# The mixer's output projection as seven half-size products for each two tiles of tokens

## What is computed

```
mix = einsum('bte,ed->btd', concat([pool_out, mlstm_out], -1), w_out)   # (512+8) x 1024 @ 1024 x 1024
x   = layer_norm(ALPHA * x + mix, ln1_g, ln1_b)
```

## Time and profile before

| what | value |
|---|---|
| median of 3 executions | 668.04 us (667.41 to 669.69) |
| profiled execution | 667.49 us |
| its span, first to last instruction | 665.8 us |
| mean granted TensorE clock | 0.992 |
| busy: PE, DVE, POOL, ACT | 96%, 52%, 31%, 23% |
| output projection on PE | 248.31 to 306.40 us |

### The profile page before, as it was taken

How to read it: one execution, slowest core, us unless ns; L and a number is a source line. 1 busy time by engine, 2 the same in 40 slices (tenths; PEclk the granted TensorE clock), 3 DMA queues, 4 the chain that set the end, 5 groups by cost and what they waited for, 6 DMA issues and landing times.

```text
span 665.8 us, 8667 instructions
## 1 busy us (share of the span) xinstructions
PE 637.3 (96%) x3244; PEld 390.3 (59%) x3244; DVE 348.1 (52%) x799; ACT 152.0 (23%) x333; POOL 208.7 (31%) x245
## 2 busy tenths in 40 slices
PE   6999999999999999999999999999999999999982
PEld 3445588887787774446888774454574454333330
DVE  0283356326457792757653865355873333253445
ACT  1113221001524230002001740222324111211144
POOL 4241010100476556411101985002244342111231
PEclk9999999999999999999999999999989999999997
DMA  8994468613334345102904987454449999999698
GB/s 296 399 324 165 143 163 223 234 52 127 99 126 164 103 158 171 40 0 84 359 0 144 336 287 310 192 189 189 194 167 371 412 413 410 382 360 410 210 207 165
DMA packets 45811, 146.14 MB, mean 220 GB/s; under 512 B 5738, under 2 KB 6058, under 8 KB 41663
## 3 DMA queue, kind: packets, MB, share of 16 engines
q1 hardware_dynamic: 31559, 107.50, 42.7%
q0 software_dynamic: 12032, 33.29, 17.7%
q10 hardware_dynamic: 2176, 4.76, 2.0%
HBM read 130.34 MB, written 20.33 MB: 226 GB/s over the span
## 4 chain that ended last, share of the span: by engine, by line
PE 87%; DMA 5%; DVE 3%; ACT 1%; issue 1%; POOL 0%; ACTq 0%; DVEq 0%; POOLq 0%
PE ps L602 15%; PE ps L749 14%; PE ps L1089 12%; PE ps L511 9%; PE ps L477 8%; PE ps L1109 5%; PE ps L600 4%; DMA xn<-y_d 3%; PE ps L850 2%; PE ps L774 2%; PE ps L658 2%; PE ps L976 1%; PE ps L834 1%; PE ps L1070 1%; PE ps L673 1%; PE ps L539 1%
## 5 line engine op out<-in xcount | busy, mean ns | idle before, releaser
L749 PE MATMUL ps<-wring,P 128*128 128x512 f32 x224 | 99.2, 596 | 0.0
L749 PEld LDWEIGHTS ps<-wring,P 128*128 128x128 f32 x224 | 41.6, 190 | 49.1 <-issue 49.0
L1089 PE MATMUL ps<-wring,P 128*32 128x512 f32 (+1 forms) x288 | 65.0, 599 | 0.9 <-DVE P L2344 0.9
L1768 DVE SCALAR_TENSOR_TENSOR P<-ps,P 128x264 f32<-128x264 f32 (+1 forms) x70 | 28.8, 426 | 61.0 <-PE ps L602 44.3
L511 PE MATMUL ps<-wring,P 128*128 128x512 f32 x128 | 58.7, 617 | 1.0 <-DVE P L1723 0.8
L477 PE MATMUL ps<-xT,wring 128*128 128x312 f32 (+1 forms) x256 | 56.8, 383 | 0.0
L2505 POOL TENSOR_SCALAR rstd<-agg 128x1 f32<-128x1 f32 (+1 forms) x15 | 16.8, 1121 | 114.5 <-DVE agg L1708 114.5
L477 PEld LDWEIGHTS ps<-xT,wring 128*128 128x128 f32 x256 | 46.6, 190 | 9.3
L2344 DVE COPY P<-ps 128x512 f32<-128x512 f32 x11 | 7.6, 692 | 75.0 <-PE ps L1070 75.0
L511 PEld LDWEIGHTS ps<-wring,P 128*128 128x128 f32 x128 | 24.9, 198 | 31.6 <-issue 31.3
L1089 PEld LDWEIGHTS ps<-wring,P 128*32 128x32 f32 (+1 forms) x288 | 22.2, 130 | 36.0 <-issue 36.0
(11 more groups left out here) (444 smaller groups left out, 1103.5 us busy)
## 6 DMA issues: line engine op xcount, KB each, us to landing
wring<-in_w_in SPq DMA_DIRECT2D x5, 2048.0 KB, 9.8
wring<-in_w_gate SPq DMA_DIRECT2D x10, 1024.0 KB, 9.1
wring<-in_w_up SPq DMA_DIRECT2D x10, 1024.0 KB, 11.6
P<-in_w_down SPq DMA_DIRECT2D x10, 1024.0 KB, 11.4
P<-in_cache_mem_k SPq DMA_DIRECT2D x8, 1024.0 KB, 6.2
P<-in_cache_mem_v SPq DMA_DIRECT2D x8, 1024.0 KB, 4.9
y_d<-P POOLq DMA_DIRECT2D x1, 4160.0 KB, 32.0
wring<-in_ca_wv SPq DMA_DIRECT2D x2, 2048.0 KB, 19.6
```

The lines of the kernel that those rows point to most:

```text
L749: last = mm(bk[:, :], src[:, k, START[t]:START[t] + TR], w[:, k, :], start=(k == 0), stop=(k == KC - 1))
L1089: last = mm(GU[p % 2][lo:lo + m, :].rearrange("p (g f) -> p g f", g=2), xgT[:, p % 3, k, lo:lo + m], gu[s][:, :, k, :], start=(k == 0), st ...
L1768: V.scalar_tensor_tensor(dst, src, scale, part, ALU.mult, ALU.add).then_inc(part_added, 1)
```

## The change

Two tiles of tokens, t and u (0 and 1, then 2 and 4), times the four 512x512 quarters of `w_out` are made with seven products of 4 matmuls each instead of eight. The products need sums of weight quarters (numbered 5, 6, 7 and 4) and sums of token blocks (5, 6, 3, 7). The weight sums are made by transfers: SP loads one quarter plainly, POOL adds another to it with an accumulating DMA. The token sums are made on DVE. The block of sum 6 lies in ring buffer 2, so wq0 is loaded only after the second pair's sixth product. Three (then one) copies of a bank from PSUM to SBUF come onto ACT before its copies of the transposed rows. The sums of token blocks for pair 0 and 1 stand right behind `take_heads(3)` on DVE. The diff, cut to its core:

```diff
+        wo_sums = {7: block_at(2144), 5: block_at(4224), 6: wring[:, 2, 0:4, :], 4: block_at(8384)}
+        PAIRS = ((0, 1), (2, 4))
+        MIXED_BANKS = (0, 1, 3, 4, 0), (1, 3, 4, 0, 1)
+        WX = [ps[6], ps[7], ps[3], ps[4], ps[5]]
...
@@ tensor
+            def mixed_product(bank, x, w, done, order=range(4), ready=None, between=None):
+                for k in order:
+                    if ready:
+                        pe.wait_ge(act_free, ready[k])
+                    if between and k == between[0]:
+                        between[1]()
+                    last = mm(bank[:, :], x[:, k, :], w[:, k, :], start=(k == order[0]), stop=(k == order[-1]))
+                last.then_inc(done, 1)
...
+            use_block("wo0")
+            at["first", 0] = mixed_product(WX[0], mixed(0, 0), wo0[:, 0:4], done=act_full, order=(2, 3, 1, 0), ready=copied)
+            at["first", 1] = mixed_product(WX[1], mixed(2, 0), wo0[:, 0:4], done=act_full, between=(2, turn_last_head))
+            for i in range(2):
+                late = lambda: pe.wait_ge(dve_free, at["heads", 3])
+                at["second", i] = mixed_product(WX[3 + i], mixed(PAIRS[i][0], 1), wo0[:, 4:8], done=dve_full, between=(3, late))
+            def mixed_pair(i, banks, after_fifth=None, after_seventh=None):
+                b, s = PAIRS[i][1], mixed_sums[i]
+                sixth, fifth, third, seventh, fourth = banks
+                pe.wait_ge(xsum_done, MIXED[i] + 2)
+                pe.wait_ge(wsum_made, T2_MADE)
...
+                at["sixth", i] = mixed_product(sixth, s[6], wo_sums[6], done=dve_full)
...
+                at["fifth", i] = mixed_product(fifth, s[5], wo_sums[5], done=act_full)
...
+                at["third", i] = mixed_product(third, s[3], wo1[:, 4:8], done=dve_full)
...
+                at["seventh", i] = mixed_product(seventh, s[7], wo_sums[7], done=dve_full)
...
+                at["fourth", i] = mixed_product(fourth, mixed(b, 1), wo_sums[4], done=dve_full)
+            mixed_pair(0, [WX[i] for i in MIXED_BANKS[0]])
             transpose_x(0, x1_ready)
...
+            mixed_pair(1, [WX[i] for i in MIXED_BANKS[1]], after_fifth=lambda: transpose_x(1, x1_ready), after_seventh=turn_sample_heads)
+            used[BI["u"]] = (dve_full, at["sixth", 1])
+            samples_mixed = at["sample heads"]
             transpose_x(2, x1_ready)
             pe.wait_ge(dve_free, samples_mixed)
             rows_samples(WO, mixT)
@@ sync
-            for i in range(3, BI["wc0"] + 1):
+            for i in range(3, BI["wq0"]):
+                block_load(i)
+            low, high = [[w[:, 0:4], w[:, 4:8]] for w in (BLOCKS[BI["wo0"]][1], BLOCKS[BI["wo1"]][1])]
+            sp.wait_ge(dve_full, at["keys", 3])
+            sp.dma_start(wo_sums[5], low[0]).then_inc(piece_in[0], 16)
+            sp.dma_start(wo_sums[7], high[0]).then_inc(piece_in[1], 16)
+            sp.wait_ge(act_full, at["u", 0])
+            sp.dma_start(wo_sums[6], high[1]).then_inc(piece_in[2], 16)
+            sp.wait_ge(dve_full, at["state", 3])
+            sp.dma_start(wo_sums[4], low[1]).then_inc(wsum_raw, 16)
+            for i in range(BI["wq0"], BI["wc0"] + 1):
                 block_load(i)
@@ scalar
+            copy_part(first_part[0], WX[0])
+            copy_part(first_part[1], WX[1])
+            copy_part(fifth_part, WX[MIXED_BANKS[0][1]])
+            take_x(0)
+            act.wait_ge(dve_free, at["fourth", 0])
+            copy_part(fifth_part, WX[MIXED_BANKS[1][1]])
+            take_x(1)
@@ vector
+            def product_of(key, bank):
+                nf[0] += 1
+                assert nf[0] == at[key]
+                dve.wait_ge(dve_full, nf[0])
+                return bank[:, :]
+            quarter_of = lambda t, q: xn[:, t, q * 512:q * 512 + 512]
+            def sum_mixed(i, products):
+                (t, u), s, done = PAIRS[i], mixed_sums[i], MIXED[i]
+                for p in products:
+                    if p == 5:
+                        V.tensor_tensor(s[5], mixed(u, 0), mixed(u, 1), ALU.subtract).then_inc(xsum_done, 1)
...
+            def take_first(i):
+                dve.wait_ge(act_free, at["first", i])
+                x = quarter_of(PAIRS[i][0], 0)
+                link(V.scalar_tensor_tensor(x, x, ALPHA, first_part[i], ALU.mult, ALU.add))
+            def take_second(i):
+                x = quarter_of(PAIRS[i][0], 0)
+                V.tensor_tensor(x, x, product_of(("second", i), WX[3 + i]), ALU.add).then_inc(dve_free, 1)
+            def take_sixth(i):
+                V.tensor_tensor(sum_part, product_of(("sixth", i), WX[MIXED_BANKS[i][0]]), first_part[i], ALU.add).then_inc(dve_free, 1)
+                dve.wait_ge(dve_free, nf[0])
+                x = quarter_of(PAIRS[i][0], 1)
+                link(V.scalar_tensor_tensor(x, x, ALPHA, sum_part, ALU.mult, ALU.subtract))
+            def take_third(i):
+                x = quarter_of(PAIRS[i][0], 1)
+                dve.wait_ge(act_free, at["fifth", i])
+                link(V.tensor_tensor(x, x, fifth_part, ALU.add))
+                V.tensor_tensor(x, x, product_of(("third", i), WX[MIXED_BANKS[i][2]]), ALU.add).then_inc(dve_free, 1)
+                dve.wait_ge(dve_free, nf[0])
+            def take_seventh(i):
+                u = PAIRS[i][1]
+                V.tensor_tensor(all_part, product_of(("seventh", i), WX[MIXED_BANKS[i][3]]), sum_part, ALU.add).then_inc(dve_free, 1)
+                dve.wait_ge(dve_free, nf[0])
+                x = quarter_of(u, 1)
+                link(V.scalar_tensor_tensor(x, x, ALPHA, all_part, ALU.mult, ALU.subtract))
+                link(V.tensor_tensor(x, x, fifth_part, ALU.add))
+                statistics(u, 1)
+                x = quarter_of(u, 0)
+                link(V.scalar_tensor_tensor(x, x, ALPHA, all_part, ALU.mult, ALU.add))
+            def take_fourth(i):
+                x = quarter_of(PAIRS[i][1], 0)
+                V.tensor_tensor(x, x, product_of(("fourth", i), WX[MIXED_BANKS[i][4]]), ALU.add).then_inc(dve_free, 1)
+                dve.wait_ge(dve_free, nf[0])
...
+            sum_mixed(0, (5, 6, 3, 7))
+            take_first(0)
+            take_first(1)
+            take_second(0)
+            dve.wait_ge(dve_free, nf[0])
+            statistics(0, 0)
+            sum_mixed(1, (5, 6, 3, 7))
+            take_second(1)
+            take_sixth(0)
             dve.wait_ge(gb_in, 32)
-            residual(0, x1_ready)
+            take_third(0)
+            norm(0, x1_ready, first_known=True)
             carried(7)
-            residual(1, x1_ready)
+            take_seventh(0)
+            take_fourth(0)
+            norm(1, x1_ready, first_known=True, last=0)
...
-            residual(2, x1_ready)
+            statistics(2, 0)
+            take_sixth(1)
+            take_third(1)
+            norm(2, x1_ready, first_known=True)
+            take_seventh(1)
...
-            residual(4, x1_ready, between=[lambda n=n: sum_weights("wq0", n) for n in (1, 2, 3)])
+            for n in (1, 2, 3):
+                sum_weights("wq0", n)
+            take_fourth(1)
+            norm(4, x1_ready, first_known=True, last=0)
             residual_samples("mixed rows", x1_ready)
@@ gpsimd
             state_out(2)
+            pool.wait_ge(piece_in[0], 32)
+            pool.dma_start(wo_sums[5], high[0], accum_op=ALU.add).then_inc(wsum_made, 16)
+            pool.wait_ge(piece_in[1], 32)
+            pool.dma_start(wo_sums[7], high[1], accum_op=ALU.add).then_inc(t3_made, 16)
             update_state(4)
+            window_sums()
             update_state(5)
-            window_sums()
+            pool.wait_ge(piece_in[2], 32)
+            pool.wait_ge(wsum_made, P_MADE)
+            pool.dma_start(wo_sums[6], wo_sums[5], accum_op=ALU.add).then_inc(wsum_made, 16)
             load_state(6)
             head_rstd(3, TR, NQT)
+            pool.wait_ge(wsum_raw, 16)
+            pool.wait_ge(wsum_made, T2_MADE)
+            pool.dma_start(wo_sums[4], wo_sums[6], accum_op=ALU.add).then_inc(wsum_made, 16)
             state_out(3)
             update_state(6)
```

More of the change, by code:

```diff
@@ L762, in _ @@
             WO = ("wo0", "wo1")
[L763 to L781, removed]
+            wo0, wo1 = [wring[:, BI[name] % WR] for name in WO]
+            def mixed_product(bank, x, w, done, order=range(4), ready=None, between=None):
[6 more added lines that the diff above has]
+                last.then_inc(done, 1)
+                count = na if done is act_full else nd
+                count[0] += 1
+                return count[0]
@@ L789, in _, with turn_sample_heads @@
[L789 to L796 removed]
+            nd[0] += 1
+            at["cq"] = nd[0]
+            def turn_sample_heads():
+                pe.wait_ge(samples_dve, HEADS_READY)
+                pe.wait_ge(dve_free, at["cq"])
+                for h in range(H):
+                    last = nc.tensor.transpose(WX[2][:, h * NS:h * NS + NS], vsn[:, h * 128:h * 128 + 128], ident[0:NS, 0:NS])
```

(26 more changed lines are left out.)

73 lines of the change are left out of this document (55 added, 18 removed).

## The result

The changed kernel takes **675.15 us** (median of 4 runs, 674.82 to 676.44), the kernel before 667.72 beside it: ratio **1.0108, 95% interval 1.0076 to 1.0141**, slower by 7.4 us where +2.7 was forecast. That is 0.15 us past the upper end of the range (675.0). The sign and the main mechanism (DVE's fixed list) were right, the size was not.

What follows compares the result with a forecast made beforehand. PE bound the kernel, with DVE only 1.35 us ahead. The sum was -0.4 (PE's saving against DVE's list) + 2.1 (state update beside DVE) + 1.0 (POOL's queue) = +2.7 us, 670.8 for the median; range 665.8 to 675.0.

Steps and rivals of the forecast that it cites:

- PE's 6.86 us: In the changed stage, 128 matmul records become 112 on PE; 16 records at 0.429 us go.
- DVE's list: From pair 0's third product to wq0's token sums, DVE's fixed order ends at 326.4, leaving a 0.4 us gain.
- Addition s: Last head delayed by POOL's queue (state 5's store, state 6's load), shifting the third product: 0 to 3 us, taken 1.0.
- ACT's four copies stand where it was idle: The new copies on ACT, 23% busy, were claimed to cost nothing.
- Addition c: update_state(7) on POOL slows DVE's seventh-product operations beside it: 0 to 2.4 us, taken 2.1.
- What was to be seen: Signs include PE waiting 4 to 6 us before tile 2's transposes and sample rows, whose norm ends at 320 to 323.
- Rival D: TensorE's clock falls in pauses around the sample rows, costing up to 7.3 us more: 674, chance 0.05.
- the forecast's case: DVE's list takes PE's gain and two additions delay the stage: 670.8 for the median, span 667.6 to 673.1, chance 0.57.
- Rivals A and B: First: DVE's list 2 us shorter, 662 at best, chance 0.16. Second: no change, 667.6, chance 0.11.
- Rival C: Accumulating transfers land late in POOL's queue, delaying state 6's load: about 4 us more, 675, chance 0.11.
- The gain or delay at the sixth product goes through to the end: From wq0's sixth product on, PE's work stays as it was, so any shift there reaches the end.

Runs made afterwards that it cites:

- e2: The changed kernel without its four accumulating transfers, the plain loads of the weight quarters kept: 671.57 us, ratio 1.0052.
- e8: The changed kernel with POOL's queue in order of need, the last output state's store and ln1 vectors placed between accumulations: 671.60 us, ratio 1.0064.
- e5: The changed kernel with unused matmuls on PE where it waits for DVE, before tile 2's transposes and the sample rows: 674.17 us, ratio 1.0101.
- e10: e8 with three additions of each pair of tiles moved from DVE to identity matmuls on PE: 668.54 us, ratio 1.0007.
- e12: e8 with two additions of the first pair moved to PE and DVE's waits filled with operations of its list: 666.30 us, ratio 0.9977.
- e1: The changed kernel with POOL's first two accumulating transfers moved behind update_state(4): 680.81 us, ratio 1.0185.
- e6: The changed kernel with the arithmetic of update_state(7) on POOL cut to a few elements: 673.76 us, ratio 1.0096.
- e9: The changed kernel with three additions of each pair moved from DVE to identity matmuls on PE, queue order as before: 671.63 us, ratio 1.0062.
- e4: The changed kernel with the first two accumulations behind update_state(4) and the last head taken ahead of state 6: 677.87 us, ratio 1.0149.
- e3: The changed kernel with the last head's 1/std right after update_state(5) and the head taken before carried(6): 676.04 us, ratio 1.0116.

## Why the prediction was right, and where it was off

- **PE's 6.86 us and DVE's list: right.** The records went and the list took the gain: 54.7 us against 53.6 plus c. e2 and e8 are still slower than before with little left but the list and the clock behind its waits, e5 shows DVE's sums as what PE waits for once the clock is held, and e10 and e12, with the list cut, get back to the time of before.
- **Addition s: the term that was mis-sized.** Taken as 1.0, bounds 0 to 3; measured 4.2 on PE (third product done 38.0 us after the landmark instead of 33.7) and 4.5 at DVE's first operation with it. The step that failed is the working of s: it follows state 5's store and the last head, and nothing else. The path that held PE is not in it: state 4's store behind two accumulations, 8.7 us to land; ACT's copies of the pooled blocks, 6.00 us of wait for that store; PE, 3.44 us for ACT. "ACT's four copies stand where it was idle" did not help to find it: the late copies are older ones ahead of those four. The head, which I did price, cost 0.56 us behind that wait (and 6.75 in e1, where the wait is gone). The third accumulation was to be issued at 246 and to land at 253 to 256. It was issued at 249.00, for POOL stood 2.58 us for its plain load, and landed at about 257: rate (186 to 219 GB/s against 201) and time to landing were right, the start was not. The Trainium skill (DMA: Bandwidth & Descriptors, "Anatomy of one DMA — SWDGE (gpsimd) path") gives, as an estimate by its fit, 4.4 us for 1 MB; the accumulations of after took 7.1 to 10.9.
- **Addition c:** 2.1 taken, 1.4 measured (e6), inside its bounds.
- **What was to be seen:** PE waits 1.7 + 2.9 = 4.7 us ahead of tile 2's transposes and the sample rows (4 to 6 forecast), the seventh's operations take 1.03 and 1.42 (1.2), the sample rows' norm ends at 324.1 (320 to 323; later by s). The last head is turned at 256.17 (254 to 256).
- **Rival D, at 0.05, happened beside the forecast's case**, at a third of its full price: 2.2 us on the sample rows, of which 0.7 came through. Its time of 674 did not follow from its own terms: 670.8 and up to 7.3 are 678. I had named the 5 us of waiting myself and took the earlier trace rows as evidence against; there PE's longest pause was 1.0 us, here they are 1.7 and 2.9. The Trainium skill (TensorE: Matmul & The Clock Gate, "HAM oscillation") tells how waits between matmuls bring the lower clock, and the trace agrees: 1.25 us busy in 305 to 310 with the granted clock at 0.76, then 0.56.
- **Rivals A and B** did not hold: without c the list is 53.3 us, 0.3 shorter than added up, where A wanted 2, and neither s nor c was 0.
- **Some luck is in the total.** The forecast's own case ended at 673.1, so the time is outside it. That it comes within 0.15 us of the stated range is owed to room that was left for C at its far end, not to s.
- **Rival C** did not hold in the kernel itself (PE never waited for a weight sum), but its mechanism, the queue, did.
- **"The gain or delay at the sixth product goes through to the end": nearly.** +6.1 there, and between 475 and 505 us come 2.6 more, by the clock (0.50 in 500 to 505; in the kernel before 0.73 in 495 to 500). It need not come with the change: e2, e8 and e10, which have the change too, take 34.0 us for that stretch, e9 35.7, before 34.7, after 37.3, with the same instructions. Each of these is one profiled execution; how often after loses it is not shown.

The stage in three parts, in us: from the first landmark to the start of DVE's list (its first operation with the third product), the list up to the start of its last row, and from there to PE's sixth product of wq0:

| run | start | list | PE behind | between landmarks |
|---|---|---|---|---|
| forecast, without s and c | 33.7 | 53.6 | 0 | 87.4 (before: 87.7) |
| after | 38.2 | 54.7 | 0.8 | 93.7 |
| e2 | 34.6 | 54.7 | 1.4 | 90.7 |
| e5 | 40.0 | 54.7 | 0.1 | 94.8 |
| e8 | 34.1 | 56.0 | 1.1 | 91.2 |
| e9 | 40.7 | 50.6 | 0.8 | 92.1 |
| e10 | 35.1 | 51.6 | 0.1 | 86.9 |
| e12 | 34.6 | 51.2 | 1.0 | 86.7 |

So after's stage is -0.3 (the forecast's list alone) + 4.5 (s) + 1.1 (the list: c's 1.4, less 0.3) + 0.8 (PE behind DVE, 0.7 of it by the clock, e5) = 6.1 us longer than before.

## What to carry over

Fewer products pay only if the engines that put the parts together have the time in their *longest fixed list*, not on average; count that list from the first result it needs to the last one it must deliver. A 1 MB transfer that accumulates is not a small edit to a queue: look up what each buffer's next user waits for (stores too), and place each transfer behind everything that is needed sooner. And when a bound moves back and forth between two engines, price both sides of each trade: an addition cost 0.7 us on DVE and 0.86 on TensorE.

## What the runs showed of the hardware that I had not expected

- 1 MB accumulating transfers keep the DMA engines full at about 200 GB/s (186 to 219 in after) and land in 7.1 to 10.9 us in after; in other runs some took longer (median of two 13.6 in e1 and 14.7 in e4, one 13.0 in e8). A 256 KB store issued beside two of them took 8.7 us.
- The granted clock fell behind a wait of about 3.5 us in some runs (3.51 in e3, 3.44 in e5; also 4.43 in e9, all at 245 to 255 us) and not in others (3.44 in after, ten records in 2.41 us; 3.21 in e6). What decides it stays open.
- What makes the later fall, at 490 to 510 us, come or stay away from run to run is open too. Against the 34.0 us of e2, e8 and e10 it costs 0.7 us in the profiled run of before and 3.3 in that of after, as much as some of the effects that were looked for here.
